# One wide product per high weight tile, and VectorE sums the halves of the bank

## The chip, the cores and the metric

The kernel runs on one core of a Trainium2 chip. The metric is the device time of one execution in microseconds. All times below are of this core; the profile is of one execution.

## What is computed

Two transformer blocks over 256 tokens of width 2048, all in fp32. The first: an RMS norm, a projection to q, k, v, gates, cross-attention queries and z; a causal convolution over four tokens and silu on q, k, v; a gated delta rule over 24 value heads in chunks of 64; cross-attention to 256 memory rows; a gate with silu(z); an output projection with residual. The second: a projection, a pooling mixer, an indexer that picks 64 keys per query, attention, an output projection, a layer norm, and a PEER layer: queries pick 16 of 16384 experts for each of 8 heads, and the output is a sum over experts.

```
h = rms_norm(x, norm_g);  proj = h @ dn_w_in
mix = deltanet(proj...);  xa = memory_cross_attention(...)
x = x + (concat(mix, xa) * silu(z)) @ w_out
proj = x @ w_in_2;  mix = concat(pool_mixer, sparse_attention) @ w_out_2
h = layer_norm(ALPHA * x + mix)
q = h @ wq; s = q . sub_keys; top 16 of 128 twice, top 16 of 256 sums, softmax -> gate
ffn = sum over experts of gate * gelu(h . u_e) * v_e
out = layer_norm(ALPHA * h + ffn)
```

## The kernel before, in words

**Units.** All large weights are cut into 466 units of 128 output columns x 2048 input rows (1 MB). The tables at L90 number them by stage: KV 0 to 15, AB 16, XQ 17 to 24, QK 25 to 48, VZ 49 to 104, WO 105 to 136 (two units for each output tile), KIWI 137, QI 138 to 145, KQ 146 to 161, V2 162 to 169, PU 170 to 177, WO2 178 to 193, WQ 194 to 209, and PEER 210 to 465: two halves, each of 64 u units and 64 value units. A value unit is another kind (`vm`): 24 products of 512 columns with the weights as the moving operand.

**Precision.** A weight half-unit of 128 x 1024 is split: ScalarE casts raw to its high part WH (`hi_part`, L1998 to 2004, rounded to fp32r), VectorE subtracts it from raw for the low part WL (`lo_part`, L1426 to 1430). X is kept as a high and a low tensor too. For each of the 16 k-tiles of a unit TensorE makes three products of 256 columns into columns 0 to 255 of one PSUM bank: WH with X high, WH with X low, WL with X high (`unit_mm`, L985). Four slots hold high and low half-units: `prep(q)` prepares half q + 3 when half q is about to be multiplied. `hi_part(q)` waits for the raw load and for TensorE to be done with half q - 4; `lo_part(q)` waits for the high part. The SP queue loads raw units three deep and waits for the low part of the unit that a load overwrites.

**Order.** Each engine runs its own program in order. One planner, class `Plan`, calls the steps of all engines in one fixed order, so a step's place in the plan is its place in each engine's queue. `unit` (L171) calls `prep(2n)`, half the products in parts, `prep(2n+1)`, the other half; it yields after each part (four yields a unit, eight with per=6), and other work is put there. After the unit comes its output step.

**Output steps.** The bank is n % 2 nearly everywhere, so two banks alternate; `feed` (L858) lists for every stage what TensorE waits for before it writes a bank again. Most output steps are a ScalarE copy from PSUM (mk, mv, ab, xq, qi, kq, v2, pu, qe), or a silu (z) or gelu (u) that reads PSUM. The convolution of q, k and v reads PSUM on VectorE (`conv`, L1543: four dependent operations), and silu follows on ScalarE. x1 and r1 are VectorE additions from PSUM.

**Stages named below.** In WQ units, after the unit, `qs_out`: ScalarE copies the query tile, TensorE multiplies it with the sub-keys, ScalarE copies the scores to ST; from WQ unit 5 on, VectorE does three `key_top` searches (L1806) in each unit, 32 in all: one after each of the first two parts, and one after the third, behind the second `lo_part`. In the first peer half the selection (`select`) is put among the first 33 u units at SEL_RATE 0.22 steps a part; then up to two steps a unit of `g_hots` (VectorE), `g_mm` (TensorE) and `g_apply` (VectorE), in the second half one. The output step of a u unit is `u_out`: gelu of PSUM to GT for the token columns whose gates are there already (GpSimd multiplies them into C3), and gelu to C3 for the rest. The delta stage (`mix`, units VZ) runs two groups of heads at a time through some 40 short steps that pass TensorE, VectorE, ScalarE and GpSimd, with quarter units between them.

Of the kernel before, what the change touches and what calls it, by code (L numbers as in the profile page):

```python
# [10 lines left out]
ALU = mybir.AluOpType  # L11
# [80 lines left out]
NUNIT = 466  # L92

# [452 lines left out]
def gate_counts():  # L546
# [9 lines left out]
    "projected": (("mk", 8), ("mv", 8), ("ab", 1), ("xq", 8), ("qi", 8), ("kq", 16), ("v2", 8), ("pu", 8), ("qe", 16)),  # L556
    "residual": (("x1", 16), ("r1", 16)),
# [4 lines left out]
    "small_dve": (("sg_min", 1), ("sg_g", 1), ("sg_gc", 2), ("keep", 1), ("bias_v", 1), ("ki", 1), ("ki_copy", 1), ("wi", 1),  # L562
# [32 lines left out]
def build(nc, D, out, scratch):  # L595
    ctx = ExitStack()
    with ctx:
# [85 lines left out]
        HH, HL, MH, ML = r(0, 4096), r(16, 4096), r(32, 4096), r(48, 4096)  # L683
# [69 lines left out]
        YH, YL = r(0, 8192), r(88, 8192)  # L753
        Y_SRC = []
        o = 0
# [5 lines left out]
        Y3, W3 = k3(YH), k3(YL)  # L761
        X1, X1H, X1L = f(32, 4096), r(48, 4096), r(64, 4096)
# [8 lines left out]
        XH2, XL2 = r(104, 4096), r(120, 4096)  # L771
# [14 lines left out]
        H2H, H2L = r(0, 4096), r(16, 4096)  # L786
# [49 lines left out]
        def tensor_program(e):  # L836
            p = Lane(e)
            last_gelu = {}
# [19 lines left out]
            def feed(n):  # L858

                hx, mx, yx = (k3(HH), k3(HL)), (k3(MH), k3(ML)), (Y3, W3)  # L860
                x1, x2, h2 = (k3(X1H), k3(X1L)), (k3(XH2), k3(XL2)), (k3(H2H), k3(H2L))
                if n < 8:
                    if n >= 2:
                        p.wait_ge(*at("mk", n - 1))
                    return *mx, n % 2, True, True
                if n < 16:
                    i = n - 8
                    p.wait_ge(*at("mk", 7 + min(i, 1)))
                    if i >= 2:
                        p.wait_ge(*at("mv", i - 1))  # L870
                    return *mx, i % 2, True, True
                if n == AB_:
                    p.wait_ge(*at("mv", 7))
                    return *hx, 0, True, True
                if n < QK_:
                    i = n - XQ_
                    p.wait_ge(*at("n_lo", 32))
                    p.wait_ge(*at("mv", 8))
                    if i:
                        p.wait_ge(*at("ab", 1))  # L880
                    if i >= 2:
                        p.wait_ge(*at("xq", i - 1))
                    return *hx, (i + 1) % 2, True, True
                if n < VZ:
                    i = n - QK_
                    p.wait_ge(*at("xq", 8 if i % 2 == 0 else 7))
                    if i >= 2:
                        p.wait_ge(*at("conv", i - 1))
# [1684 lines left out]
```

## Time and profile before

| | |
|---|---|
| median of 3 runs | 3459.13 us (3459.13 to 3462.56) |
| the profiled execution | 3462.52 us |
| its span | 3460.7 us |
| TensorE busy | 3308.0 us |
| VectorE busy | 1999.7 us |
| ScalarE busy | 1439.5 us |
| mean granted TensorE clock | 0.979 |

The span goes from the first to the last instruction; what lies around it is 1.8 us. Busy times are unions over the instructions of an engine. Matmuls are pipelined: a busy TensorE may still stand waiting inside, so the distance between starts tells more than the duration. Waits in the trace are put down to the event that came last. One line, L841, makes nearly all products, and L1989 nearly all ScalarE functions, so groups are told apart by their operands.

### The profile page before, as it was taken

To read this page: it belongs to the slowest core of one execution; us is meant where nothing else is said; L and a number is where in the kernel's file an instruction comes from. 1 tells how busy PE (TensorE), PEld (TensorE's weight loads), DVE (VectorE), ACT (ScalarE), POOL (GpSimd) and SP (SyncE) were. 2 spreads that over 40 slices of the span, in tenths; PEclk is the share of its full clock that TensorE was granted. 3 is DMA by queue.
4 is the path that set the end of the run, shared out by engine and by line. 5 is a ranking of instruction groups with operands and counts; after the bars stand their busy time and mean duration, and the time that the engine had idled before them with its cause. 6 is when DMAs were issued, how large, how long until landed. Compare 5 with 4: busy or idle time off the path is not lost.

```text
span 3460.7 us, 56098 instructions
## 1 busy us (share of the span) xinstructions
PE 3308.0 (96%) x23976; PEld 3123.7 (90%) x23976; DVE 1999.7 (58%) x3459; ACT 1439.5 (42%) x2131; POOL 292.5 (8%) x331
## 2 busy tenths in 40 slices
PE   7999999999899999999989999999999999999996
PEld 6999988989898999999979999998888999998885
DVE  5456655545444444655468877875555666655554
ACT  5445345435344433443354443334444333334443
POOL 0000022122123000004000000000000000000000
PEclk9999999999999999999999999999999999999998
DMA  5434322222221454444434543445555444455553
GB/s 189 160 140 147 134 72 88 86 74 98 71 77 37 148 187 168 170 159 161 153 139 159 178 182 137 144 146 192 192 192 184 159 159 159 160 212 191 191 193 119
DMA packets 70825, 511.05 MB, mean 148 GB/s; under 512 B 7912, under 2 KB 8048, under 8 KB 10032
## 3 DMA queue, kind: packets, MB, share of 16 engines
q1 hardware_dynamic: 67968, 491.81, 39.8%
q0 software_dynamic: 1456, 11.27, 0.9%
q8 instruction: 190, 3.11, 0.4%
q10 hardware_dynamic: 1152, 4.37, 0.3%
q14 instruction: 59, 0.48, 0.0%
HBM read 503.15 MB, written 4.21 MB: 147 GB/s over the span
## 4 chain that ended last, share of the span: by engine, by line
PE 85%; DVE 6%; ACT 6%; issue 2%; DMA 1%; POOL 0%; SPq 0%; ACTq 0%; DVEq 0%; POOLq 0%
PE PS L841 85%; ACT WH L2004 2%; DVE WL L1430 2%; ACT m L1989 2%; DVE m L1421 2%; ACT L1989 1%; ACT m L1990 0%; DMA raw<-in_w_kv 0%; PE PS L844 0%; DVE m L1424 0%; DVE m L1449 0%; ACT m_4096r L1989 0%; DVE m_4096r L1421 0%; DVE m L1618 0%; DVE m L1616 0%
## 5 line engine op out<-in xcount | busy, mean ns | idle before, releaser
L841 PE MATMUL PS<-m_4096r,WH 128*128 128x256 f32 x9792 | 1856.3, 290 | 28.4 <-DVE m_4096r L1421 10.3
L1430 DVE TENSOR_TENSOR WL<-raw,WH 128x1024 fp32r<-128x1024 f32 x932 | 1152.9, 1239 | 1109.0 <-ACT WH L2004 1107.3
L841 PEld LDWEIGHTS PS<-m_4096r,WH 128*128 128x128 f32 x9792 | 1543.1, 194 | 51.8 <-issue 20.9
L841 PE MATMUL PS<-m_4096r,WL 128*128 128x256 f32 x4896 | 1395.6, 285 | 0.0
L2004 ACT CAST WH<-raw 128x1024 fp32r<-128x1024 f32 x932 | 973.9, 1047 | 979.6 <-PE PS L841 975.4
L841 PEld LDWEIGHTS PS<-m_4096r,WL 128*128 128x128 f32 x4896 | 947.9, 194 | 0.0
L841 PE MATMUL PS<-WH,m_512r 128*128 128x512 f32 x2048 | 549.9, 390 | 4.0 <-DVE m_512r L1932 4.0
L841 PEld LDWEIGHTS PS<-WH,m_512r 128*128 128x128 f32 x2048 | 385.8, 188 | 84.6 <-issue 4.3
L841 PE MATMUL PS<-m 128*128 128x128 f32 (+5 forms) x2512 | 363.2, 287 | 45.0 <-ACT m L2163 14.1
L841 PEld LDWEIGHTS PS<-m 128*128 128x128 f32 (+2 forms) x2512 | 316.0, 187 | 72.5 <-ACT m L2163 16.5
L841 PE MATMUL PS<-WL,m_512r 128*128 128x512 f32 x1024 | 316.4, 390 | 0.0
L841 PEld LDWEIGHTS PS<-WL,m_512r 128*128 128x128 f32 x1024 | 193.0, 188 | 40.1
L1989 ACT ACTIVATE m<-PS 128x256 f32<-128x256 f32 (+32 forms) x296 | 83.4, 320 | 305.7 <-PE PS L841 292.4
L841 PE MATMUL PS<-m_8192r,WH 128*128 128x256 f32 x1024 | 186.6, 285 | 2.8 <-issue 2.8
L841 PEld LDWEIGHTS PS<-m_8192r,WH 128*128 128x128 f32 x1024 | 161.6, 194 | 3.0 <-issue 3.0
L841 PE MATMUL PS<-m,m 128*128 128x64 f32 (+4 forms) x1170 | 153.1, 278 | 9.7 <-ACT m L2195 3.7
L841 PEld LDWEIGHTS PS<-m,m 128*128 128x128 f32 (+1 forms) x1170 | 142.3, 192 | 13.2 <-ACT m L2195 5.3
L2488 POOL TENSOR_TENSOR m<-m,m 128x8 f32<-128x8 f32 (+30 forms) x92 | 43.5, 472 | 1243.8 <-ACT m L1989 1243.8
L1898 DVE TENSOR_SCALAR m<-cons,m 128x128 f32<-128x128 f32 x512 | 148.4, 354 | 0.0
L841 PE MATMUL PS<-m_8192r,WL 128*128 128x256 f32 x512 | 145.8, 285 | 0.0
L1989 ACT ACTIVATE m<-m 128x256 f32<-128x256 f32 (+5 forms) x104 | 50.2, 501 | 173.9 <-DVE m L1421 145.0
L841 PEld LDWEIGHTS PS<-m_8192r,WL 128*128 128x128 f32 x512 | 99.4, 194 | 0.0
(178 smaller groups left out, 1743.3 us busy)
## 6 DMA issues: line engine op xcount, KB each, us to landing
raw<-in_pu SPq DMA_DIRECT2D x128, 1024.0 KB, 4.8
raw<-in_pv SPq DMA_DIRECT2D x128, 1024.0 KB, 5.3
raw<-in_w_qkv SPq DMA_DIRECT2D x48, 1024.0 KB, 4.8
raw<-in_w_o SPq DMA_DIRECT2D x48, 1024.0 KB, 4.8
raw<-in_w SPq DMA_DIRECT2D x40, 1024.0 KB, 4.8
raw<-in_w_z SPq DMA_DIRECT2D x32, 1024.0 KB, 4.8
raw<-in_w_kv SPq DMA_DIRECT2D x16, 1024.0 KB, 4.8
raw<-in_w_q SPq DMA_DIRECT2D x16, 1024.0 KB, 4.8
```

Of the source, the lines that this page charges most:

```text
L841: return e.matmul(o, l, x, start=start, stop=stop)
L1421: return e.scalar_tensor_tensor(out=o, in0=a, scalar=s, in1=b, op0=op0, op1=op1)
L1430: tt(WL[:, k, :], raw[:, n % NRAW, h * 1024:h * 1024 + 1024], WH[:, k, :].bitcast(F), ALU.subtract).then_inc(S["lo"], 1)
L1898: ts(O1[:, ob, k, :], C("iota"), I1T[:, t:t + 1], GTT[:, t:t + 1], ALU.is_equal, ALU.mult)
L1989: return e.activation(o, i, fn, scale=scale, bias=bias)
L2004: e.copy(WH[:, k, :], raw[:, n % NRAW, h * 1024:h * 1024 + 1024]).then_inc(S["hi"], 1)
L2488: tt(C3[:, j, 0:tq], C3[:, j, 0:tq], half_of(GT, j % 2)[:, 0:tq], ALU.mult).then_inc(S["gated"], 1)
```

## The change

For each k-tile, WH is multiplied once with a moving operand of 512 columns: X high and X low side by side, written to the whole bank. WL with X high is added to columns 0 to 255. Odd k-tiles make the narrow product first. VectorE sums the two halves of the bank where the output is taken out (`total`), in place of ScalarE; silu, gelu and the scale of q then run on ScalarE from SBUF, behind it. x1 and r1 take two dependent VectorE operations. The banks now alternate over all outputs (`output`, `bank`), `feed` waits for the reduce of the output two before, and all these semaphores are joined in one chain.

```
+            def total(o, n, first=0, last=256):
+                both = PS[:, bank(n), :].rearrange("p (s t) -> p t s", s=2)
+                return e.tensor_reduce(o, both[:, first:last, :], AX.X, ALU.add)
...
-                    mm(PS[:, bank, 0:256], wh, XH[:, x, :], start and x == 0, False)
-                    mm(PS[:, bank, 0:256], wh, XL[:, x, :], False, False)
-                    t = mm(PS[:, bank, 0:256], wl, XH[:, x, :], False, stop and x == 15)
+                    xs = X(first + x)
+                    if x % 2 == 0:
+                        mm(PS[:, b, :], wh, xs, start and x == 0, False)
+                        mm(PS[:, b, 0:256], wl, xs[:, 0, :], False, False)
+                    else:
+                        mm(PS[:, b, 0:256], wl, xs[:, 0, :], False, False)
+                        t = mm(PS[:, b, :], wh, xs, False, stop and x == 15)
...
+                if output(n) >= 2:
+                    p.wait_ge(*at("mk", output(n) - 1))
```

On VectorE (the outputs mk, mv, ab, xq, qi, kq, v2, pu, ki and z have the manner of `qs_out`, v that of `qk_out`, and x1 that of `r1_out`):

```
+            def qs_out(i):
+                v.wait_ge(*at("used", done(WQ + i)))
...
+                total(f(76 + i % 4, 256), WQ + i).then_inc(S["qe"], 1)
+            def qk_out(i):
+                x = tile(QT if i % 2 else KT, i // 2)
...
+                total(x, QK_ + i).then_inc(S["qk"], 1)
+                v.wait_ge(*at("qk", i + 1))
+                conv(i, i // 2 if i % 2 else 12 + i // 2, x)
             def u_out(half, j, tq):
+                v.wait_ge(*at("used", done(n)))
+                if tq:
...
+                    x = total(half_of(GT, j % 2)[:, 0:tq], n, 0, tq)
                 if tq < 256:
...
+                    x = total(C3[:, j, tq:256], n, tq, 256)
+                x.then_inc(S["u"], 1)
             def r1_out(m):
+                v.step(stt(tile(X1, m), tile(X1, m), ALPHA, PS[:, b, 0:256], ALU.mult, ALU.add))
+                v.own()
+                tt(tile(X1, m), tile(X1, m), PS[:, b, 256:512], ALU.add).then_inc(S["r1"], 1)
```

On ScalarE:

```
             def qs_out(i):
-                a.wait_ge(*at("used", done(WQ + i)))
...
-                e.copy(f(76 + i % 4, 256), PS[:, i % 2, 0:256]).then_inc(S["qe"], 1)
                 a.wait_ge(*at("qs", i + 1))
             def z_out(n, i):
+                a.wait_ge(*at("vz", n + 1))
+                act(z_tile(i), z_tile(i), ACT.Silu).then_inc(S["z"], 1)
             def u_out(half, j, tq):
+                a.wait_ge(*at("u", 64 * half + j + 1))
                 if tq:
+                    act(gt[:, 0:tq], gt[:, 0:tq], ACT.Gelu).then_inc(S["gelu_gated"], 1)
                 if tq < 256:
+                    act(C3[:, j, tq:256], C3[:, j, tq:256], ACT.Gelu).then_inc(S["gelu"], 1)
```

## Rows read from the trace of the kernel before

**Rows 1.** The page: busy time of each engine, and what was read from memory.

```profile
PE 3308.0 (96%) x23976; PEld 3123.7 (90%) x23976; DVE 1999.7 (58%) x3459; ACT 1439.5 (42%) x2131; POOL 292.5 (8%) x331
...
HBM read 503.15 MB, written 4.21 MB: 147 GB/s over the span
```

**Rows 2.** The waits: who waited for whom, us in total, times, longest.

```profile
DVE WL L1430 <- ACT WH L2004: 1107.3, 770, 19.6
```

**Rows 3.** TensorE's timeline (start, us, what), at the full clock and (from 1349) the low one.

```profile
1200.06 0.40 PE L841 MATMUL PS<-m_8192r,WH 128*128 128x256 f32 x2
1200.30 0.28 PE L841 MATMUL PS<-m_8192r,WL 128*128 128x256 f32 x1
1200.42 0.40 PE L841 MATMUL PS<-m_8192r,WH 128*128 128x256 f32 x2
...
1349.42 0.63 PE L841 MATMUL PS<-m_4096r,WH 128*128 128x256 f32 x2
...
1350.06 0.63 PE L841 MATMUL PS<-m_4096r,WH 128*128 128x256 f32 x2
```

**Rows 4.** TensorE's timeline in a value unit: four and two products of 512 columns.

```profile
2500.27 1.07 PE L841 MATMUL PS<-WH,m_512r 128*128 128x512 f32 x4
2501.18 0.62 PE L841 MATMUL PS<-WL,m_512r 128*128 128x512 f32 x2
2501.63 1.07 PE L841 MATMUL PS<-WH,m_512r 128*128 128x512 f32 x4
```

**Rows 5.** Stretches: length, PE, PEld, DVE, ACT, POOL busy, clock, DMA share, GB/s.

```profile
202.70:377.10 174.40, 168.84 (x1304) 165.65 (x1304) 118.38 (x193) 86.66 (x115) 17.70 (x24) 0.96 0.40 144
377.10:1157.80 780.70, 723.80 (x5618) 686.99 (x5618) 372.62 (x609) 330.28 (x560) 179.44 (x141) 0.96 0.22 77
1797.20:1873.40 76.20, 71.11 (x575) 68.88 (x574) 69.04 (x262) 30.17 (x44) 0.00 (x0) 1.00 0.49 176
1873.40:2067.60 194.20, 191.27 (x1594) 190.87 (x1593) 156.56 (x300) 85.02 (x106) 0.00 (x0) 1.00 0.50 177
2067.60:2301.10 233.50, 233.50 (x1985) 233.44 (x1984) 188.06 (x488) 75.15 (x122) 13.84 (x29) 1.00 0.40 142
2696.70:2763.10 66.40, 66.40 (x562) 66.40 (x561) 42.09 (x90) 24.29 (x40) 2.66 (x10) 1.00 0.45 159
```

**Rows 6.** Groups by form on VectorE: busy us, mean ns, and idle before.

```profile
L1864 DVE TENSOR_REDUCE m<-m 128x128 f32<-128x2048 f32 x4 | 9.1, 2280 | 0.0
L1527 DVE TENSOR_REDUCE m<-PS 128x1 f32<-128x256 f32 x8 | 3.4, 420 | 2.2 <-PE PS L841 2.2
```

**Rows 7.** ScalarE's timeline at the end of a WQ unit: query copy, scores, high part.

```profile
1824.03 0.37 ACT L2272 COPY m<-PS 128x256 f32<-128x256 f32 x1 [1.77 <-PE PS L841]
1825.21 0.37 ACT L2274 COPY m<-PS 128x256 f32<-128x256 f32 x1 [0.80 <-PE PS L841]
1825.48 1.05 ACT L2004 CAST WH<-raw 128x1024 fp32r<-128x1024 f32 x1
```

**Rows 8.** VectorE's timeline in the same unit: low parts, and the searches' first rows.

```profile
1824.09 1.21 DVE L1430 TENSOR_TENSOR WL<-raw,WH 128x1024 fp32r<-128x1024 f32 x1
1825.21 0.29 DVE L1797 MAX8 m<-m 128x8 f32<-128x128 f32 x1
...
1826.79 1.21 DVE L1430 TENSOR_TENSOR WL<-raw,WH 128x1024 fp32r<-128x1024 f32 x1
...
1831.07 1.21 DVE L1430 TENSOR_TENSOR WL<-raw,WH 128x1024 fp32r<-128x1024 f32 x1
```

**Rows 9.** Groups by form on ScalarE: a function of 256 columns from SBUF.

```profile
L1989 ACT ACTIVATE m<-m 128x256 f32<-128x256 f32 x64 | 26.4, 417 | 166.4 <-DVE m L1421 145.0 <-DVE m L1771 21.4
```

**Rows 10.** ScalarE's timeline at the end of a hot unit: two gelus, high part.

```profile
2128.02 0.45 ACT L1989 ACTIVATE m<-PS 128x56 f32<-128x56 f32 x2 [2.66 <-PE PS L841]
2128.35 1.05 ACT L2004 CAST WH<-raw 128x1024 fp32r<-128x1024 f32 x1
```

More of the change, by code:

```diff
@@ L92, with output, bank @@
 NUNIT = 466
+def output(n):
+    if n < WO:
+        return n
+    if n < KIWI:
+        return WO + (n - WO) // 2
+    if n < PEER:
+        return n - 16
+    half, j = divmod(n - PEER, 128)
+    return PEER - 16 + 64 * half + j
+def bank(n):
+    return output(n) % 2
 def fill_order():
@@ L680, in build, with high_low, pair @@
             units += [D["pu"][64 * half + j] for j in range(64)] + [vv[64 * half + j] for j in range(64)]
-        HH, HL, MH, ML = r(0, 4096), r(16, 4096), r(32, 4096), r(48, 4096)
+        def high_low(kb, tiles, apart):
+            both = r(kb, apart * 256 + tiles * 256)
+            row = both.ap[0][0]
+            def pair(x):
+                return bass.AP(both.tensor, both.offset + x * 256, [[row, 128], [apart * 256, 2], [1, 256]])
+            return both[:, 0:tiles * 256], both[:, apart * 256:(apart + tiles) * 256], pair
+        HH, HL, H_X = high_low(0, 16, 16)
+        MH, ML, M_X = high_low(32, 16, 16)
         XT, TMP, MT = f(64, 4096), f(80, 4096), f(96, 4096)
@@ L872, in feed @@
[L872 to L876, printed above, removed]
-                    p.wait_ge(*at("n_lo", 32))
[L878 to L888, printed above, removed]
-                    return *hx, i % 2, True, True
@@ L942, in feed @@
+                if n < AB_:
+                    return M_X, 0, True, True
+                if n < WO:
+                    p.wait_ge(*at("n_lo", 32))
+                    return H_X, 0, True, True
+                if n < KIWI:
+                    second = (n - WO) % 2
+                    return Y_X, 16 * second, not second, bool(second)
+                if n < WO2:
+                    p.wait_ge(*at("x1_lo", 16))
+                    return X1_X, 0, True, True
                 if n < WQ:
-                    i = n - WO2
@@ L957, in feed @@
-                half, j = divmod(n - PEER, 128)
-                if j < 2:
-                    if half:
-                        p.wait_ge(*at("acc_v" if j == 0 else "acc_a", 1))
-                    else:
-                        p.wait_ge(*at("qe", 15 + j))
-                else:
-                    p.wait_ge(*last_gelu[128 * half + j - 2])
-                return *h2, j % 2, True, True
+                    return X2_X, 0, True, True
+                if PEER + 128 <= n < PEER + 130:
+                    p.wait_ge(*at("acc_a" if bank(n) else "acc_v", 1))
@@ L967, in arrived @@
+                return H2_X, 0, True, True
             def arrived(n, x):
@@ L987, in unit_mm @@
                     now[0] = feed(n)
-                XH, XL, bank, start, stop = now[0]
+                X, first, start, stop = now[0]
+                b = bank(n)
                 k = (n % 2) * 2 + h
```

273 lines of the change are left out of this document (95 added, 178 removed).

## The prediction, made before the changed kernel was run

> **What bounds the kernel now.** I read the page first: TensorE is busy 96% of the span, VectorE 58%, ScalarE 42% [rows 1]. That looks like a kernel bound by TensorE, with VectorE free to take work. Two more views bend this. The waits show VectorE waiting 1107 us in 770 places for ScalarE's high parts [rows 2], so its idle time is not free time: it sits at the head of a queue whose next instruction needs ScalarE. And the table by stretch shows that VectorE's work is uneven: 69.0 of 76.2 us in the last eleven query units (WQ 5 to 15), 156.6 of 194.2 in the first 33 units of the first peer half (the selection), 188.1 of 233.5 in its other 31 [rows 5].
>
> **The gain: one product fewer per k-tile.** At the full clock three 256-column products start 0.36 us apart as a set, so 120 ns each [rows 3]. Six 512-column products take 1.36 us, so 226.7 ns each [rows 4]. 256 columns at 2.4 GHz are 106.7 ns, 512 are 213.3: both rows leave 13.3 ns per product, whatever its width. A k-tile goes from 360 ns to 226.7 + 120 = 346.7, a unit of 16 k-tiles from 5.76 to 5.55 us (0.213 less). At the low level of 1.2 GHz three products take 0.64 us [rows 3], 213 each, which is all columns, and nothing is gained there. There are 338 such units (466 less the 128 value units), so 72 us is the ceiling. The new moving operand is two runs of 256 columns far apart; no row shows such a read. Bounds: 226.7, as a 512 run, and 240, as two products; I take 226.7, since the columns are the same number.
> A rule speaks against the size: the Trainium skill, TensorE: Matmul & The Clock Gate, section Back-to-back issue gap, gives a fixed 2.5 ns per product at the full clock. By it the merge would return 2.5 ns per k-tile, 14 us in all instead of 72. The rows contradict it.
>
> **What the sum of halves costs.** The copy on ScalarE (0.37 us [rows 7]) becomes a reduce on VectorE over 512 elements in pairs. Reduces over 256 from PSUM take 420 ns, over 2048 from SBUF 2280 [rows 6]: 1.04 ns per element and 153 fixed, so 0.69 us; in a full queue some 0.6, as neighbours overlap by 0.1. Where it is cut in two (u with a gated part) 0.74. Bounds: 0.42 (a 256 read) and 0.85 (two of them). I take 0.69.
> But VectorE's order decides. After the reduce of unit n-1 its next instruction is the low part 2n+3, which waits for the high part 2n+3, which ScalarE makes after its own step of unit n-1. Before, that step waited for TensorE alone. Now it waits for the reduce, and VectorE stands idle behind it: a loop VectorE, ScalarE, VectorE once a unit. Where VectorE has time to spare this costs nothing. Where it has not, each unit pays the reduce and the idle time.
>
> **Query units 5 to 15.** Now the low parts of successive units start at 1824.09 and 1831.07, 6.98 us apart, filled without a gap: two low parts of 1.12 and three key searches of 1.58 [rows 8]. TensorE's period is 76.2/11 = 6.93 [rows 5]. The high part meanwhile runs 2 us ahead. After: the reduce, then TensorE's score products, the copy to ST, the high part, then the low part. Read from ScalarE's rows: copy ends 1824.40, high part ends 1826.53 [rows 7], so 2.15 us from the end of the reduce to the low part. Loop: 0.72 + 2.15 + 6.98 = 9.85 us against 6.93, 11 units, less 1.6 because 32 searches fill 11 units but for one: **+31**. TensorE then pauses 3.5 us in each of these units. Should the granted clock fall in the pauses and stay low, a unit takes 16 x 0.64 = 10.2 us [rows 3] and TensorE closes a loop of 11.4 with the reduce and the score products: some 17 us more at worst, which I leave to the range.
>
> **The selection, 33 units.** VectorE's own work is 156.6 us [rows 5]. Added per unit: 0.6 of reduce and 1.5 of idle (gelu from SBUF 0.42 [rows 9], high part 1.05 [rows 7], less an overlap of 0.1, three hand-overs). 156.6 + 33 x 2.1 = 226; 3 for gaps between dependent operations, 5 for the two softmax exchanges with ScalarE, where VectorE has nothing to do in either kernel, less 2.5 left over from the searches: 231.5, against 194.2: **+37**. It could be 25 if some idle time that the trace has already is the same wait.
>
> **The hot units, 31.** Period 233.5/31 = 7.53, VectorE 188.1/31 = 6.07 [rows 5]. Added: 0.65, then 0.05 + 0.39 (two gelus) + 1.05 + 0.03 = 1.52; two gelus and the high part take 1.38 from PSUM now [rows 10]. 6.07 + 0.65 + 1.52 = 8.24 against 7.53: 0.71 x 31 = **+22**.
>
> **Everywhere else TensorE sets the pace.** 338 - 11 - 64 = 263 units, 4208 k-tiles at 13.3 ns = 56 us; the granted clock is 0.96 to 1.00 there [rows 5], so some 4% of them run low: **-54**. What is given back, **+22**:
> - TensorE waits for the evacuated tile right after the unit in KI, 8 QI and WQ 0 to 4: 0.69 in place of 0.37, 14 x 0.32 = 4.5.
> - Ends of stages, where the next products need the last tile (x1 and r1 now take two adds of 0.43, c_begin, kq with its extra scaling): 8 x 0.45 = 3.5.
> - The 24 q/k units: convolution, silu, high part, low part already make a loop near 5.8 us; VectorE works 118.4/24 = 4.93 a unit of 7.27 [rows 5]. With 0.6 more the last ones run at 6.4: +3.
> - The delta stage: VectorE works only 373 of 781 us, but TensorE idles 57 [rows 5], so part of it hangs on chains through VectorE. 56 reduces, a quarter of them on the chain: +9. From 0 to 56 x 0.8.
> - The second peer half has one hot step a unit: period 66.4/10 = 6.64, VectorE 4.21 [rows 5]. After: 4.21 + 0.65 + 1.52 = 6.38 for VectorE, 6.43 for TensorE. It just fits; 2 for where it doesn't.
> Value units (128) and their splits are untouched. The DMA queue waits for the low parts only; 147 GB/s over the span [rows 1] leaves it room. GpSimd gets its gelu some 0.8 us later and idles there.
>
> **Sum:** -54 + 22 + 31 + 37 + 22 = +58, on the profiled execution's 3462.5 us (span 3460.7): 3520. The three runs lie at 3459.1 and 3462.6 with a median of 3459.1, so I put the figure at 3518.
>
> **Rivals.**
> - *The loops don't bind* (faster, 0.06). If the wait of the low part falls into time in which VectorE would idle anyway, only its work counts: 11 + 17 saturated units x 0.65 = 18, plus 8 for the waits of TensorE, less 70: 3418. It decides at the first query units with searches: a period under 7.1 us there means this one. Against it: those searches leave VectorE no gap [rows 8]. For it: the high parts run far ahead now, and in the selection VectorE idles 38 us, some of which may absorb it.
> - *The loops reach the delta and q/k stages too* (0.13). ScalarE's silu of z waits behind VectorE's chain work, and the chain behind both: 56 x 0.8 = 45 instead of 9, with 3 more in q/k: 3560.
> - *The pair of runs costs 240 ns* (0.04). The change then doesn't do what it says and term -54 is lost: 3572.
> - *A product's fixed part is small, so that merging returns a fifth* (0.01). Both rows show 13.3 ns [rows 3, 4], so it would have to be the columns that get slower in a pair: 10 us instead of 54, 3562. This is the case by the Trainium skill, TensorE: Matmul & The Clock Gate, Back-to-back issue gap (2.5 ns, 4208 times).
> - *My mechanism, as summed* (0.76): own range 3490 to 3545 (reduce 0.42 to 0.85 over 75 units, -20 to +12; selection -12).
>
> **Numbers.** 3518; 3485 to 3560 takes in the likeliest case with its bounds and most of the second rival. A measurement tells some 0.2% (7 us) from no change: faster 0.06, same 0.02, slower 0.92.
>
> **What would show it.** Right: products pair up at 346 to 347 ns per k-tile in WO and the second peer half; low parts in WQ 5 to 15 start some 9.8 us apart, VectorE idle for 2 us after each reduce, released by ScalarE's high part; TensorE idle there some 3 us a unit; selection near 230 us, hot units at 8.2; second peer half at 6.45. Wrong: a query period under 8 us, or a hot unit at 7.3, breaks the loop argument; a k-tile at 360 breaks the gain; a longer delta stage (over 790 us) the estimate of its chains.

## The result, and the profile after

The changed kernel takes 3569.22 us (median of 4 runs, 3565.64 to 3570.49), against 3460.85 us for the kernel before (4 runs, 3459.13 to 3465.96, the three runs stated above among them): a ratio of 1.0309, 95% interval 1.0291 to 1.0327. The forecast was 3518, with a range of 3485 to 3560: the direction was right, the change was +108 us where +58 was forecast, and the time lies above the range. The stretches and rows below come from one profiled execution of each kernel; that of the changed kernel took 3570.49 us.

First the page of the changed kernel (busy us and instructions by engine, then the shares of the chain of work that ended last, followed back from the last instruction), the same chain in the kernel before and, from the waits, the two rows that bear on the new step. L1374 is the sum of halves, L2016 holds nearly all of ScalarE's functions, L1363 and L2031 make the low and the high parts.

```profile
PE 3316.2 (93%) x18568; PEld 2856.3 (80%) x18568; DVE 2203.1 (62%) x3871; ACT 1420.6 (40%) x2058; POOL 289.0 (8%) x331
...
PE 68%; DVE 20%; ACT 8%; issue 4%; DMA 1%; POOL 0%; SPq 0%; DVEq 0%; ACTq 0%; POOLq 0%
```

The same chain in the kernel before:

```profile
PE 85%; DVE 6%; ACT 6%; issue 2%; DMA 1%; POOL 0%; SPq 0%; ACTq 0%; DVEq 0%; POOLq 0%
```

The waits in the changed kernel:

```profile
DVE WL L1363 <- ACT WH L2031: 999.1, 707, 18.9
...
ACT m L2016 <- DVE m L1374: 545.1, 146, 7.1
```

TensorE's share fell from 96% to 93% [rows 1], VectorE's busy time rose by 203 us, and VectorE's share of the chain that ended last went from 6% to 20%. ScalarE now waits 545 us for the sum. The wait of VectorE for the high part, in which the argument saw the harm, is *shorter* in total than before (999 us against 1107 [rows 2]). The total hides it: most of this idle time costs nothing in either kernel. Only the table by stretch shows where it matters. These are the stretches of [rows 5] in the changed kernel: q/k stage, delta stage, WQ units 5 to 15, selection (33 units), the other 31 u units with the end of the half, and ten units of the second peer half.

```profile
201.90:383.60 181.70, 168.13 (x922) 145.14 (x920) 129.01 (x212) 86.58 (x115) 17.71 (x24) 0.95 0.40 136
383.60:1194.90 811.30, 734.40 (x4722) 646.54 (x4722) 426.00 (x671) 330.85 (x561) 176.90 (x141) 0.94 0.22 75
1825.70:1933.00 107.30, 81.16 (x399) 68.71 (x399) 77.04 (x273) 26.08 (x33) 0.00 (x0) 0.86 0.36 125
1933.00:2169.20 236.20, 200.22 (x1066) 170.41 (x1065) 175.16 (x329) 83.57 (x106) 0.00 (x0) 0.94 0.43 144
2169.20:2423.40 254.20, 239.43 (x1506) 209.86 (x1504) 206.09 (x563) 76.04 (x126) 13.49 (x30) 0.99 0.39 132
...
2800.70:2865.50 64.80, 64.80 (x401) 57.71 (x400) 48.81 (x111) 24.98 (x40) 2.49 (x10) 1.00 0.48 163
```

Against the forecast by stage (lengths from the first product of a stage to the first of the next; the forecast column divides the sum on record, the gain among it, over the stages):

| stage | before | after | change | forecast |
|---|---|---|---|---|
| q/k, 24 units | 174.4 | 181.7 | +7.3 | -2 |
| delta, 56 units | 780.7 | 811.3 | +30.6 | -2 |
| WO, 32 units | 190.8 | 184.4 | -6.4 | -6.6 |
| WQ, 16 units | 123.9 | 158.9 | +35.0 | +32 |
| selection | 194.2 | 236.2 | +42.0 | +37 |
| rest of first u half | 238.3 | 254.2 | +15.9 | +22 |
| second u half | 428.1 | 418.1 | -10.0 | -11 |
| the other stages | | | -6 | -10 |

So 42 of the 50 us that were missed came from two stages, q/k and delta. The other terms were close, in part because errors cancel: the selection cost 5 us more than forecast and the rest of that half 6 us less.

**The gain is there.** TensorE's timeline in WO (start, us, what; each row groups two neighbouring products):

```profile
1240.42 0.62 PE L867 MATMUL PS<-m_30720r,WH 128*128 128x512 f32 x2
1240.88 0.40 PE L867 MATMUL PS<-m_30720r,WL 128*128 128x256 f32 x2
1241.12 0.63 PE L867 MATMUL PS<-m_30720r,WH 128*128 128x512 f32 x2
```

Two k-tiles start 0.70 us apart, one each 0.35, as against 0.36 before; forecast 0.347. The moving operand in two separate runs costs nothing that can be seen.

**The loop of a WQ unit is there.** VectorE's timeline, from one sum to the next (idle time before an instruction and its releaser in brackets), then ScalarE's and TensorE's around the same two sums:

```profile
1886.14 0.67 DVE L1374 TENSOR_REDUCE m<-PS 128x256 f32<-128x512 f32 x1
1888.98 1.23 DVE L1363 TENSOR_TENSOR WL<-raw,WH 128x1024 fp32r<-128x1024 f32 x1 [2.16 <-ACT WH L2031]
...
1893.27 1.21 DVE L1363 TENSOR_TENSOR WL<-raw,WH 128x1024 fp32r<-128x1024 f32 x1
...
1895.97 0.67 DVE L1374 TENSOR_REDUCE m<-PS 128x256 f32<-128x512 f32 x1
```

```profile
1887.62 0.37 ACT L2251 COPY m<-PS 128x256 f32<-128x256 f32 x1 [4.23 <-PE PS L867]
1887.89 1.06 ACT L2031 CAST WH<-raw 128x1024 fp32r<-128x1024 f32 x1
```

```profile
1886.87 0.71 PE L867 MATMUL PS<-m 128*128 128x128 f32 x4 [1.83 <-DVE m L1374]
1896.70 0.58 PE L867 MATMUL PS<-m 128*128 128x128 f32 x1 [3.53 <-DVE m L1374]
```

Sum, score products, copy, high part, low part: VectorE idles 2.16 us from the end of the sum (forecast 2.15), and from sum to sum it is 9.83 us (forecast 9.85). In eight successive units this alternates with 10.7 us (mean 10.26). At the start of a longer one TensorE has just stood for 3.53 us, and what follows runs at the low level of its clock. A stretch of products after the long wait, and one after the short wait of 1.83 us:

```profile
1896.70:1900.00 3.30, 3.30 (x12) 3.01 (x13) 0.69 (x1) 1.31 (x2) 0.00 (x0) 0.50 0.00 0
1886.90:1890.00 3.10, 3.10 (x20) 2.79 (x21) 1.02 (x1) 1.33 (x2) 0.00 (x0) 1.00 0.00 0
```

The granted clock is 0.50 (1.2 GHz) in the first, with 12 products in 3.3 us, and 1.00 (2.4 GHz) in the second, with 20 in 3.1. So TensorE closes the longer loop every second time; the forecast had this as a possibility and left it to the range. That the stretch of WQ 5 to 15 still grew by 31.1 us where 31 was forecast is in part luck: the eight units cost 3.3 us more than at 9.85 each, and the last three distances, which hold two searches each (8.25, 8.64 and 8.27 us), 2.8 us less than the forecast allowed for them.

### The profile page after: what moved, and what is told of

The parts are those of the page before. It is cut to its first block, busy times and chain, and to the rows that moved or that the text cites. A ratio compares the mean times of both kernels' runs of the same rounds, so it can differ in the third digit from the quotient of the medians.

```text
span 3568.7 us, 45612 instructions
## 1 busy us (share of the span) xinstructions
PE 3316.2 (93%) x18568; PEld 2856.3 (80%) x18568; DVE 2203.1 (62%) x3871; ACT 1420.6 (40%) x2058; POOL 289.0 (8%) x331
## 3 DMA queue, kind: packets, MB, share of 16 engines
q10 hardware_dynamic: 1152, 4.37, 0.3%
## 4 chain that ended last, share of the span: by engine, by line
PE 68%; DVE 20%; ACT 8%; issue 4%; DMA 1%; POOL 0%; SPq 0%; DVEq 0%; ACTq 0%; POOLq 0%
PE PS L867 67%; DVE WL L1363 5%; ACT WH L2031 4%; DVE m L1354 3%; DVE m L1374 2%; ACT m L2016 2%; DVE m L1912 2%; ACT L2016 1%; DVE m L1931 1%; DVE m L1913 1%; ACT m L2017 1%; PE PS L870 0%; DVE m L1357 0%; DVE m L1806 0%; DVE m L1811 0%
## 5 line engine op out<-in xcount | busy, mean ns | idle before, releaser
L1363 DVE TENSOR_TENSOR WL<-raw,WH 128x1024 fp32r<-128x1024 f32 x932 | 1154.2, 1241 | 1000.0 <-ACT WH L2031 999.1
L867 PE MATMUL PS<-m_8192r,WH 128*128 128x512 f32 x4896 | 1726.5, 417 | 45.5 <-DVE m L1374 23.6
L2031 ACT CAST WH<-raw 128x1024 fp32r<-128x1024 f32 x932 | 966.8, 1045 | 840.4 <-PE PS L867 837.4
L867 PEld LDWEIGHTS PS<-m_8192r,WL 128*128 128x128 f32 x4896 | 955.3, 195 | 203.8 <-DVE m_8192r L1354 0.5
L867 PE MATMUL PS<-m_8192r,WL 128*128 128x256 f32 x4896 | 991.8, 285 | 0.2 <-DVE m_8192r L1354 0.2
L867 PEld LDWEIGHTS PS<-m_8192r,WH 128*128 128x128 f32 x4896 | 815.6, 195 | 74.1 <-DVE m L1374 28.0
L867 PEld LDWEIGHTS PS<-m 128*128 128x128 f32 (+2 forms) x2512 | 329.9, 190 | 125.0 <-DVE m L1374 37.7
L2016 ACT ACTIVATE m<-m 128x256 f32<-128x256 f32 (+22 forms) x355 | 125.4, 383 | 753.0 <-DVE m L1374 545.1
L1374 DVE TENSOR_REDUCE m<-PS 128x256 f32<-128x512 f32 (+31 forms) x381 | 204.6, 557 | 70.8 <-PE PS L867 65.2
L867 PE MATMUL PS<-m_30720r,WH 128*128 128x512 f32 x512 | 162.7, 399 | 3.1 <-issue 2.8
L867 PEld LDWEIGHTS PS<-m_30720r,WL 128*128 128x128 f32 x512 | 97.3, 190 | 22.7
L867 PE MATMUL PS<-m_30720r,WL 128*128 128x256 f32 x512 | 101.4, 280 | 0.0
```

The lines of the kernel that those rows point to most:

```text
L867: return e.matmul(o, l, x, start=start, stop=stop)
L1363: tt(WL[:, k, :], raw[:, n % NRAW, h * 1024:h * 1024 + 1024], WH[:, k, :].bitcast(F), ALU.subtract).then_inc(S["lo"], 1)
L1374: return e.tensor_reduce(o, both[:, first:last, :], AX.X, ALU.add)
L2016: return e.activation(o, i, fn, scale=scale, bias=bias)
L2031: e.copy(WH[:, k, :], raw[:, n % NRAW, h * 1024:h * 1024 + 1024]).then_inc(S["hi"], 1)
```

## The experiments

Theory 1 was the one that the forecast had for three stages, now for all: behind an output step that waits for VectorE, ScalarE makes the next high part late, VectorE waits for it in line, and whatever stands behind it is late too. The rivals: the sum itself and the later hand-overs lie on the chains (2), TensorE's shorter units put its fill work out of step (3), the convolution's steps have become slower (4). Theories 5 and 6 came up on the way.

The medians and ratios below are against runs of the kernel before on the same chip; its own medians on the four chips used lie between 3460.76 and 3462.71 us. The stage lengths are each read from one profiled execution. They repeat to some 4 us where a stage is not touched: the first sixteen units took 118.5 to 122.9 us in three kernels that have the same code there (experiments 1, 6 and 8). A change of a stage by 5 us is therefore hardly more than what it repeats to. TensorE's idle time in a stage is the length of the stretch less its busy time.

**1. The high part first.** The move that breaks the loop and nothing else:

```
     def unit(self, n, per=12):
...
+        self.do("early", n)
...
+            def early(n):                      # ScalarE
+                q = 2 * n + 5
+                if q < 2 * NUNIT:
+                    made.add(q)
+                    hi_part(q)
             def prep(q):
...
-                    if k < 2 * NUNIT:
+                    if k < 2 * NUNIT and k not in made:
                         hi_part(k)
```

> The changed kernel, but ScalarE makes the high part 2n+5 before its output step of unit n instead of behind it; nothing else moves. Theory 1 (the loop: sum on VectorE, output step on ScalarE, high part, low part on VectorE) says that all stages get their time back: query stage 159 to about 128 us (its searching units 7.7 us apart instead of 10.25), first peer half 490 to about 432, delta stage 811 to about 780, q/k stage 182 to about 174: some 3445 in all. Theory 2 (in the delta and q/k stages it is the sum itself and the later hand-over to silu and convolution that lie on the chains, not the high part) says that the query stage and the peer half come back all the same, but the delta stage stays over 800 and the q/k stage over 179: some 3485.

Measured: 3449.1 us (ratio 0.9965, 0.9954 to 0.9977), 120 us less than the changed kernel and faster than the kernel before. The stretches of q/k, delta, WQ and the first u half:

```profile
201.80:367.20 165.40, 162.55 (x922) 142.35 (x920) 133.52 (x218) 90.09 (x116) 28.38 (x24) 0.97 0.46 156
367.20:1149.30 782.10, 721.60 (x4723) 635.08 (x4722) 419.83 (x665) 333.94 (x560) 178.20 (x141) 0.96 0.23 76
1728.20:1872.80 144.60, 121.26 (x609) 99.87 (x609) 104.75 (x308) 53.92 (x75) 0.54 (x1) 0.87 0.37 131
1872.80:2302.50 429.70, 419.12 (x2569) 370.85 (x2568) 380.06 (x891) 168.20 (x232) 30.24 (x30) 0.99 0.47 157
```

The first u half falls from 490 to 430 with the same VectorE time (380 us): all that it had lost was the idle time of the loop. Delta falls by 29 and q/k by 16, so theory 2 as it stood (over 800 and over 179) is out. WQ comes back by 14 only, where 31 were expected: something else holds it (experiment 6).

**2. The gain alone.** The kernel before, with the new products and its old output steps.

```
-                    mm(PS[:, bank, 0:256], wh, XH[:, x, :], start and x == 0, False)
-                    mm(PS[:, bank, 0:256], wh, XL[:, x, :], False, False)
-                    t = mm(PS[:, bank, 0:256], wl, XH[:, x, :], False, stop and x == 15)
+                    xs = X(base + x)
+                    if x % 2 == 0:
+                        mm(PS[:, bank, :], wh, xs, start and x == 0, False)
+                        mm(PS[:, bank, 0:256], wl, xs[:, 0, :], False, False)
+                    else:
+                        mm(PS[:, bank, 0:256], wl, xs[:, 0, :], False, False)
+                        t = mm(PS[:, bank, :], wh, xs, False, stop and x == 15)
```

> The kernel before with the merged product of the changed kernel, but with its own output steps, which read columns 0 to 255 of the bank (the products of W high with X low are left out of the results). The merge is worth 0.213 us in each of 338 units: 72 us if TensorE sets the pace in all of them, 60 to 65 where the delta stage does not pass it on; so about 3392 to 3400. Theory 3 (the delta stage grows because TensorE's shorter units put its fill work out of step with the chains, whatever VectorE does) says that the delta stage is over 795 us here too; theories 1 and 2 say 770 to 782.

Measured: 3416.27 us (0.9870, 0.9853 to 0.9886), so the gain is 44 us and not 60 to 72. Its delta stage and second u half:

```profile
373.60:1151.70 778.10, 718.57 (x4722) 633.39 (x4721) 372.56 (x611) 330.00 (x560) 179.08 (x141) 0.96 0.23 78
2623.20:3040.60 417.40, 414.95 (x2560) 369.05 (x2561) 271.21 (x580) 157.93 (x258) 30.16 (x65) 1.00 0.48 162
```

The u half gives 10.7 of 64 x 0.213 = 13.6 us, the delta stage 2.6 of 11.9, q/k 1.8 of 5.1. In the delta stage TensorE's busy time falls by 5.2 us only, and half of that turns into longer waits (59.5 us idle against 56.9). Why its busy time there falls by less than half of 11.9 was not found out. But the stage doesn't grow, so theory 3 is out.

**3. The sums alone.** The changed kernel, 14 of 16 k-tiles with three products again.

```
-                    if x % 2 == 0:
+                    if x == 0:
...
+                    elif x < 15:
+                        mm(PS[:, b, 0:256], wh, xs[:, 0, :], False, False)
+                        mm(PS[:, b, 256:512], wh, xs[:, 1, :], False, False)
+                        t = mm(PS[:, b, 0:256], wl, xs[:, 0, :], False, False)
```

> The changed kernel with three products of 256 columns in 14 of the 16 k-tiles of each unit (the second one into the upper half of the bank), so that the sums on VectorE stand almost alone. Theory 1: TensorE waits in the query stage, the selection and the hot units, so these stay as they are within 5 us; the others take 14 x 13.3 ns = 0.19 us more per unit, 255 units, +48: about 3617, and the delta stage 811 to 822. Theory 3 says that the delta stage falls below 795, because TensorE is back in its old step.

Measured: 3595.82 us (1.0393, 1.0376 to 1.0410), +27 where +48 was expected. WQ (158.3) and the first u half (490.4) don't move, as the loop argument has it. WO gives 5.7 of 6.0 and the second u half 8.6 of 11.9. The delta stage grows to 818, within what theory 1 gave and against theory 3. The rest of the stages return little; q/k is even 3.5 us shorter.

**4. A shorter step in the same place.** VectorE copies columns 0 to 255 (418 ns) in place of the sum (684).

```
             def total(o, n, first=0, last=256):
-                both = PS[:, bank(n), :].rearrange("p (s t) -> p t s", s=2)
-                return e.tensor_reduce(o, both[:, first:last, :], AX.X, ALU.add)
+                return copy(o, PS[:, bank(n), first:last])
```

> The changed kernel, but VectorE copies columns 0 to 255 of the bank in place of the sum of both halves (the products of W high with X low are left out of the results, apart from the two residual stages). The step takes about 0.42 us instead of 0.6 to 0.69. Theory 1: each unit of the loop is shorter by that, 75 x 0.25 = 19 us in the query stage and the first peer half, 3 to 5 us in all other waits; the delta stage goes down by under 5, since what it loses is the place of the step and not its size: about 3545. Theory 2: the size of the sum is on the delta chains, 56 x 0.25 = 14 us off that stage alone.

Measured: 3523.13 us (1.0185, 1.0168 to 1.0202), 46 us less than the changed kernel where 24 were expected. WQ (152.6) and the first u half (472.5) give 24 together, in place of 19. The delta stage:

```profile
370.70:1164.00 793.30, 723.05 (x4722) 636.13 (x4721) 409.53 (x671) 331.05 (x561) 178.72 (x141) 0.95 0.22 76
```

It gives 18, and q/k 9. VectorE works 16.5 us less in the delta stage. "Its place and not its size", which theory 1 had for that stage (under 5 us), is wrong; theory 2, with 14, was nearer on this point. How much of the 18 is the step's is less sure. The profiled execution is the fastest of four that spread over 12 us, 8 us under their median, and of its 18 us in the delta stage 6.7 are shorter waits of TensorE; the other 11.3 are shorter busy time, as 24 us less of that busy time ran at the low clock.

**5. The same move in the kernel before.** Is the early high part simply a better order? The edit of experiment 1, on the kernel before.

> The kernel before with the same move as early_high (ScalarE makes the high part 2n+5 before its output step of unit n). Theory 1 says that in the kernel before the output step waits for TensorE alone, so there is no loop to break: delta stage 781 +- 5, query stage and peer halves within 2 us, and only the q/k stage, where the silu waits for the convolution on VectorE, falls from 174 to about 167: some 3452. If the move is simply a better order for any kernel, and early_high's 120 us have little to do with the change, the delta stage falls below 765 here and the total below 3435.

Measured: 3472.47 us (1.0033, 1.0019 to 1.0048), 10 us slower than the kernel before. Neither side of the expectation had this: the total was to be 3452 or under 3435, and WQ was to stay within 2 us. Its q/k, delta and WQ stages:

```profile
206.30:372.80 166.50, 163.77 (x1304) 161.86 (x1305) 117.22 (x194) 91.11 (x116) 28.89 (x25) 0.99 0.42 152
372.80:1143.00 770.20, 721.44 (x5617) 684.56 (x5618) 373.46 (x608) 331.89 (x559) 180.09 (x141) 0.96 0.22 77
1741.60:1883.50 141.90, 116.94 (x864) 111.57 (x865) 96.30 (x292) 58.38 (x91) 0.55 (x1) 0.92 0.37 134
```

Delta falls by 10.5 and q/k by 8; the u halves don't move (432.9 and 429.0); WQ grows by 18, QI by 8, since now ScalarE's copy of the query tile stands behind the high part, and TensorE's score products wait for this copy:

```profile
1826.63 1.04 ACT L2005 CAST WH<-raw 128x1024 fp32r<-128x1024 f32 x1 [1.77 <-PE PS L842]
1827.58 0.37 ACT L2281 COPY m<-PS 128x256 f32<-128x256 f32 x1
```

```profile
1827.99 0.71 PE L842 MATMUL PS<-m 128*128 128x128 f32 x4 [1.41 <-ACT m L2281]
```

So of the 29 us that the move saved in the changed delta stage, some 10 are to be had without the change; by that difference the other 18 or so are the loop's. In the u half all 61 are the loop's.

**6. The second loop of the WQ units.** TensorE's program alone, on top of experiment 1:

```
                 if h == 0 and part == 0:
                     now[0] = feed(n)
+                if h == 1 and part == 0 and WQ < n <= PEER:
+                    scores(n - 1 - WQ)       # was called right after unit n - 1
```

> early_high, and TensorE makes the score products of query unit n in the middle of unit n+1 instead of right after unit n. Theory 5: what is left in the query stage of early_high (144.6 us against 123.9 before) is a second loop: TensorE stands behind these products, which wait for the sum on VectorE, which waits behind the searches. Then the units with searches go at VectorE's pace of 7.6 us or less, the query stage is 128 to 133 us and the total 3434 to 3438. If instead VectorE's own load is the limit, it stays over 140.

Measured: 3424.51 us (0.9891, 0.9874 to 0.9907), WQ at 121.2 us: more than theory 5 had hoped for (128 to 133, total 3434 to 3438), and under the 123.9 of the kernel before. VectorE's and TensorE's timelines in the searching units:

```profile
1797.48 0.67 DVE L1377 TENSOR_REDUCE m<-PS 128x256 f32<-128x512 f32 x1
...
1805.06 0.67 DVE L1377 TENSOR_REDUCE m<-PS 128x256 f32<-128x512 f32 x1
```

```profile
1798.21 0.71 PE L868 MATMUL PS<-m 128*128 128x128 f32 x4 [1.29 <-DVE m L1377]
1805.79 0.71 PE L868 MATMUL PS<-m 128*128 128x128 f32 x4 [1.28 <-DVE m L1377]
```

7.58 us a unit: two low parts, three searches and the sum, and no idle time of VectorE. What held the stage was that TensorE stood behind its score products, they stood for the sum, and the sum stood behind the searches.

**7. The convolution's operands.** In the changed kernel the convolution takes the summed tile from SBUF and its running result from SBUF too. Here the running result lies in the bank.

```
-            def conv(k, widx, x):
-                tmp = CONV[k % 2]
+            def conv(k, widx, x, tmp):
...
+                conv(v_index(i), 24 + i, tile(VT, i), PS[:, bank(VZ + n), 0:256])
...
-                act(dst, CONV[k % 2], ACT.Silu).then_inc(S["silu"], 1)
+                act(dst, PS[:, bank(n), 0:256], ACT.Silu).then_inc(S["silu"], 1)
```

> The changed kernel, but the convolution's running result lies in the unit's own bank (its columns 0 to 255, free once the halves are summed) and not in SBUF, so that its four steps have one operand in SBUF instead of two. Theory 4: beside work of GpSimd the steps with both operands in SBUF took 1.0 to 1.4 us in the delta stage and 0.48 without, which is 17 us more of VectorE there; they go back to 0.48, and the delta stage falls by 8 to 18 us, to about 798; q/k, where GpSimd does next to nothing, stays at 182: about 3556. If these steps lie beside other work, the delta stage stays within 4 us of 811.

The three dependent steps of one tile in the changed kernel, and GpSimd beside them:

```profile
569.88 4.37 DVE L1354 SCALAR_TENSOR_TENSOR m<-m,vecs,m 128x255 f32<-128x255 f32 x3
```

```profile
569.86 1.27 POOL L2356 TENSOR_TENSOR m<-m,cons 128x512 f32<-128x512 f32 x1 [3.95 <-ACT m L2159]
571.09 1.47 POOL L2357 TENSOR_TENSOR m<-m,cons 128x512 f32<-128x512 f32 x1
572.64 1.32 POOL L2359 TENSOR_TENSOR m<-m,cons 128x512 f32<-128x512 f32 x1
```

and of the same tile with the result in the bank, again beside GpSimd:

```profile
569.09 1.53 DVE L1359 SCALAR_TENSOR_TENSOR PS<-m,vecs,PS 128x255 f32<-128x255 f32 x3
```

```profile
569.23 1.28 POOL L2358 TENSOR_TENSOR m<-m,cons 128x512 f32<-128x512 f32 x1 [4.24 <-ACT m L2161]
570.47 1.29 POOL L2359 TENSOR_TENSOR m<-m,cons 128x512 f32<-128x512 f32 x1
```

Three steps take 4.37 us with both operands in SBUF and 1.53 with one. Of the 75 such steps in the changed delta stage 20 overlap with an instruction of GpSimd and take 1.22 us on average (up to 1.56), the other 55 take 0.48: 15 us more in all, where theory 4 had 17. From the bank all 75 take 0.49, 25 of them beside GpSimd. The Trainium skill, SBUF — State Buffer, section SBUF: two separate sides, says that a VectorE operation with two SBUF inputs and a GpSimd operation that reads SBUF exclude each other for a whole instruction. By that rule the steps with one input in PSUM are free of it; the trace agrees, 4.37 against 1.53 us.

For the time it is worth less than expected: 3562.22 us (1.0282, 1.0265 to 1.0299), delta 805.8, q/k 182.9. The delta stage gives 5.5 us, below the 8 to 18 of theory 4, and hardly more than what a stage repeats to; the intervals of the two kernels' ratios overlap too. So some 10 of the 15 us lie beside other work, and that the rest counts is likely, not shown.

**8. Both, on the best version so far.** The edits of experiments 6 and 7 together.

> late_scores with the convolution of conv_bank. Theory 4 says that the delta stage of early_high (782 us) falls by another 5 to 15; with the query stage at 130 the total is 3420 to 3432, under both kernels. If the high part's loop was all that made the convolution's length count, the delta stage stays at 782 and the total at 3436.

Measured: 3422.07 us (0.9877, 0.9861 to 0.9894); delta 778.7 against 782.8. Its interval overlaps that of experiment 6: a few us at most, and inside what a stage repeats to.

**9 and 10. z or v?** The changed kernel, with the sums taken out for one kind of tile in the delta stage alone.

```
             def z_out(n, i):                                     # z_direct, ScalarE
-                a.wait_ge(*at("vz", n + 1))
-                act(z_tile(i), z_tile(i), ACT.Silu).then_inc(S["z"], 1)
+                a.wait_ge(*at("used", done(VZ + n)))
...
+                act(z_tile(i), PS[:, bank(VZ + n), 0:256], ACT.Silu).then_inc(S["z"], 1)
...
             def v_out(n, i):                                     # v_direct, VectorE
-                total(tile(VT, i), VZ + n).then_inc(S["vz"], 1)
-                v.wait_ge(*at("vz", n + 1))
-                conv(v_index(i), 24 + i, tile(VT, i))
+                conv(v_index(i), 24 + i, PS[:, bank(VZ + n), 0:256])
```

> The changed kernel, but in the delta stage ScalarE takes the 32 z tiles out of the bank itself, as before, from columns 0 to 255 (their products of W high with X low are left out of the results). Theory 1 with z as its main place: before, only the 24 v tiles had a step on VectorE ahead of ScalarE's, so the 32 z units are where the loop is new; the delta stage falls from 811 by about 20, to 791. The rival (the v units, where the sum lengthens a chain of convolution, silu, high part and low part that was there already, and whose steps are slower beside GpSimd) says that it falls by 10 or less. The other stages stay as they are.

```profile
378.10:1182.00 803.90, 731.36 (x4721) 643.85 (x4722) 403.05 (x639) 330.62 (x561) 178.75 (x141) 0.94 0.22 75
```

> The changed kernel, but in the delta stage the convolution of the 24 v tiles reads columns 0 to 255 of the bank, as before, with no sum ahead of it (their products of W high with X low are left out of the results). With z as the main place the delta stage falls by about 10, to 801, of which 5 is the slower steps beside GpSimd that conv_bank measured; the rival says 20 or more, to 791 or less. The two falls, of this kernel and of z_direct, should add up to 25 to 35 if the places are independent.

```profile
383.50:1172.40 788.90, 727.22 (x4722) 640.42 (x4722) 400.10 (x647) 331.24 (x561) 177.43 (x141) 0.95 0.22 77
```

Measured: 3559.18 us without the z sums (1.0283, 1.0266 to 1.0300), 3541.63 without the v sums (1.0221, 1.0204 to 1.0239). The delta stage falls by 7 and by 22, together 29.8 of the 30.6 by which it had grown. VectorE's work falls by much the same in both (23 and 26 us). The profiled execution is the fastest of four for z and the slowest of four for v, so the stretches understate the difference: the medians fall by 10 and by 28. So the rival is right: it is the 24 v tiles, where the sum and the slower steps lengthen a chain that was there already (convolution, silu, high part, low part), not the 32 z tiles where the chain is new.

**11. z tiles half a unit later.** On top of experiment 6:

```
         for h in range(2):
+            if h:
+                self.flush()                 # the z step kept back from the unit before
             self.do("prep", 2 * n + h)
...
-            self.do("v_out" if kind == "v" else "z_out", n, i)
+            if kind == "v":
+                self.do("v_out", n, i)
+            else:
+                self.later = n, i, st["z"]
```

> late_scores, but the step of each z tile (the sum on VectorE and the silu on ScalarE) stands half a unit later in both queues. Theory 6: as VectorE takes its instructions in order, the sum of a z tile makes it wait for the end of the unit (36 us of waits for TensorE in the delta stage, which the kernel before has for the v tiles alone), and steps of the delta chains stand behind it; half a unit later that wait is gone, and the delta stage falls from 783 by 5 to 12. If the chains are not held there, it stays within 4 us; it could rise, since TensorE has half a unit less until it needs the bank. Total 3413 to 3420, or 3425.

```profile
367.40:1137.80 770.40, 711.84 (x4723) 627.85 (x4722) 418.42 (x665) 329.39 (x557) 177.84 (x141) 0.96 0.23 77
```

Measured: 3414.4 us (0.9860, 0.9844 to 0.9877), delta down by 12.4 at the same VectorE work. In the waits of this stage the sums wait 18.6 us for TensorE, 41.0 in experiment 6, whose delta stage was:

```profile
361.40:1144.20 782.80, 723.01 (x4722) 636.22 (x4721) 419.57 (x665) 333.77 (x560) 179.22 (x141) 0.95 0.22 76
```

So the place of the z step was worth 12 us of the stage's length, and 10 of the total. But the theory's reason, that steps of the chains stand behind it, is shown in part only: TensorE's idle time is nearly what it was (58.6 us against 59.8), and what fell is its busy time (711.8 against 723.0), as 21 us less of it ran at the low clock. The waits lie otherwise, and the clock falls less often (11 stretches at the low level, 15 before); which wait went away was not followed.

This kernel keeps all of the computation and is 1.4% (48 us) faster than the kernel before. Some 18 us of that, in the q/k and delta stages, the early high part gives to the kernel before too (experiment 5), and the kernel before was not run with the late score products, so the change by itself is not shown to be worth 48 us.

**12. The last two together.**

> z_later with the convolution of conv_bank. If the slower steps beside GpSimd still stand on the way of something that ends a stage late, the delta stage falls from 770 by 3 to 6 as in the two pairs measured (811 to 806, 783 to 779), and the total is 3408 to 3412. If they now lie beside other work, it is 3413 to 3417, the same as z_later.

Measured: 3413.26 us (0.9863, 0.9847 to 0.9880), delta 769.2: the same as z_later. If the slower steps cost anything here, it is less than the 3 to 6 us expected.

## Why the prediction was wrong, and what of it was right

The step that failed is the term for the delta stage, "56 reduces, a quarter of them on the chain: +9", and with it the smaller one for q/k. The forecast let the loop of VectorE, ScalarE and VectorE bind in full in the WQ units and the first u half, gave it 3 us in q/k and none in the delta stage; the runs show it in both. They grew by 31 and 7 us where -2 and -2 were forecast, which is 42 of the 50 us missed.

**Right, by its own steps.** The gain where TensorE sets the pace: WO fell by 6.4 us for 32 units where 6.6 was forecast; the ten-unit stretch of the second u half fell by 1.6 (66.4 to 64.8), where 13.3 ns per k-tile would have been 2.1. Two runs of 256 columns cost no more than one of 512. The sum: 684 ns where 690 was read off [rows 6]. The loop in WQ: 9.83 against 9.85 us, the idle time of 2.16 against 2.15. The selection +42 against +37, the hot units and the end of the half +16 against +22 (their period is some 8.05 us, forecast 8.24). Experiment 1 shows the cause and not only the size: one instruction moved on ScalarE takes the u half from 490 to 430. The WQ stage came to +35 against +32, but for two reasons of which one was forecast as the mechanism and the other only as a bound: with the high part's loop broken it still stood at 144.6, because TensorE waited in line for the sum behind the searches. That term was right by its number more than by its whole cause. One of its readings was off, without harm to the sum: "the high part runs 2 us ahead" holds for every second high part alone. The one in the loop ends at 1826.53 and its low part starts at 1826.79 [rows 7, 8], 0.26 us later, so nothing was left there to absorb a delay.

**Wrong: the term for the delta stage**, +9 less 12 of gain. It measured +31. The runs show these causes; they overlap and don't add up to 31:
- The loop. With the high part ahead of the output step (experiment 1) the stage falls by 29 us, of which the kernel before gets 10.5 from the same move; some 18 are the loop's.
- Which tiles. The second rival's 56 x 0.8 thought of z. It was mostly the v tiles (22 of 30 us), where the sum stands ahead of four dependent steps. These steps also became slower through their new operands in SBUF, by 15 us of VectorE's time, which the forecast did not cost at all. In the stage's length 5.5 us of that were read (experiment 7), hardly clear of what a stage repeats to.
- The gain itself. The forecast let every TensorE-bound unit return 0.213 us and counted the delta's 56 among these. Alone, the stage gives back 2.6 us of 11.9 (experiment 2).
- The clock. TensorE's idle time rose by 20 us, from 56.9 to 76.9, and 35 us more of the stage ran at the low clock (63 and 98 us in the trace's record of the clock). The forecast priced a wait at its own length.

TensorE in the delta stage of the kernels that have the merged product (us; the last column is how much of the stage the clock was at its low level):

| kernel | length | idle | busy | low clock |
|---|---|---|---|---|
| changed | 811.3 | 76.9 | 734.4 | 98 |
| no z sums (9) | 803.9 | 72.5 | 731.4 | 94 |
| shorter step (4) | 793.3 | 70.2 | 723.1 | 74 |
| no v sums (10) | 788.9 | 61.7 | 727.2 | 82 |
| high part first (1) | 782.1 | 60.5 | 721.6 | 70 |
| gain alone (2) | 778.1 | 59.5 | 718.6 | 63 |
| z half a unit later (11) | 770.4 | 58.6 | 711.8 | 55 |

The products are the same in all seven, and yet TensorE is busy for 712 to 734 us with them: the more of the stage at the low clock, the longer. Of the 33 us between the gain alone and the changed kernel 17 are waits and 16 are this.

**Wrong: the term for q/k**, +3 less 5 of gain. It measured +7.3. TensorE's idle time there went from 5.6 to 13.6 us, and with the high part moved ahead the stage falls by 16.3, of which the kernel before gets 8 from the same move; the other 8 are what the loop had added. And the gain came back at 1.8 of 5.1 only. The rival "the loops reach the delta and q/k stages too", given 0.13 and 3560, is nearest to what happened: by it the delta stage changes by 45 - 12 = +33 (measured +31) and q/k by +1 (measured +7). It named z's silu as the place, though, and the runs show mostly v; that its +33 comes so near is luck in part.

**The -54** itself: 44.5 us came back over all 338 units when no sums stood in the way, of a ceiling of 72; the u halves and WO return most of theirs, the delta stage and q/k little. By the Trainium skill, TensorE: Matmul & The Clock Gate, section Back-to-back issue gap, whose formula adds a fixed 2.5 ns to a product at the full clock, it would have been 14, by an estimate from that figure; the measurement decides against it for these fp32r products.

The likeliest case stood on busy shares by stage. For the delta stage, where VectorE's share was 48%, it lacked a look at which instructions depend on each other and who stands behind them; the share said nothing on the cost of a longer step.

**What stays open.** The falls of experiments 4, 9 and 10 don't fit one rate: 0.3 us for each us of VectorE's work on z, 0.9 on v, over 1 for the shorter step on all of them. Part of it is how often the clock falls, and what decides that in this stage was not found. Which one of the delta chain's steps ends each of TensorE's waits was not followed further. The two loops of the WQ stage were not broken one by one in the other order, since late score products without the early high part would make a loop of their own.

## What to carry to other kernels

When an output step gets a predecessor on another engine, write down what stands behind it in both queues: here one copy moved ahead of a step took back 120 us, while the same copy moved in the kernel without the new dependence cost 10. Count a saving of TensorE's in the stages where TensorE sets the pace; the one that waits for chains returned a fifth. In a stage of short dependent steps don't price what is added by the engine's idle share: here each us of VectorE's work cost between 0.3 us (z) and 0.9 us (v), and about half of what the stage lost to the sums was TensorE running at the low clock and not waiting.

## What the runs showed of the hardware that was not expected

- Convolution steps on VectorE with two operands in SBUF took 1.22 us on average (up to 1.56) beside GpSimd and 0.48 alone; with one of the two in PSUM 0.49, GpSimd or not.
- After a TensorE wait of 3.53 us the products ran at a granted clock of 0.50 for over 3 us, after one of 1.83 us at 1.00. In the delta stage 20 us more of waiting came with 35 us more at the low clock; but experiment 11 took away 19 us at the low clock with nearly the same waiting in total (58.6 us against 59.8).
- A moving operand of 512 columns in two runs of 256, far apart, was read at the pace of a single run (0.35 us for the wide and the narrow product together).
